# Layer 0 transposes x as it lands and applies its inverse norm behind the projection; x, identity and a gain share one tensor

## The chip, the cores and the metric

The kernel runs on one core of a Trainium2 chip. The metric is the device time of one execution in microseconds (us); lower is better.

## The reference

Four residual layers over 256 tokens of width 1024, everything in float32. Each layer is a token mixer (forgetting attention in layers 0 and 3, chunk attention with a position bias in layer 1, sliding-window attention with sinks in layer 2), a gated MLP with a causal convolution, and a gated per-layer embedding. What matters here is the beginning of layer 0:

```python
def rms_norm(x, g):
    xf = x.astype(jnp.float32)
    y = xf * lax.rsqrt(jnp.mean(xf * xf, axis=-1, keepdims=True) + EPS)
    return (y * g.astype(jnp.float32)).astype(x.dtype)

    h = rms_norm(x, attn_norm[i])
    # fox_mixer
    proj = h @ w_in
    q = rms_norm(proj[..., :D].reshape(B, S, N_HEADS, HEAD_DIM), qn)
    k = rms_norm(proj[..., D:2 * D].reshape(B, S, N_HEADS, HEAD_DIM), kn)
    v = proj[..., 2 * D:3 * D].reshape(B, S, N_HEADS, HEAD_DIM)
    log_f = jax.nn.log_sigmoid((proj[..., 3 * D:] + b_f).astype(jnp.float32))
```

The inverse norm of a token is one number per row of x, so it can be multiplied in before the projection or behind it; the gain belongs to the columns of x and so to the contraction.

## The kernel before

**Arithmetic.** A float32 product is made of three products of rounded operands: each operand is split into a rounded part (`hi`, float32r) and the rest (`lo`), and PE adds hi x hi, hi x lo and lo x hi (`three`, L1409 to L1411). So every weight is rounded by ACT (`split_hi`, L460) and its rest is made by DVE (`split_lo`, L805); the same is done to the transposed activations hT.

**Weights.** They come as units of 128 x 2048 (1 MB) in the order of use, each as two halves of 128 x 1024. SP loads halves into the ring `w_raw` of 4; a slot is free when DVE has made the rest of the half in it (`lo_ready`, the loop at L432 to L436). `w_hi` and `w_lo` are rings of 4 units.

**Order.** There is no scheduler. Each engine has its instructions in the order in which its function is written, and semaphores join them. An engine waits at the first instruction whose semaphore is late, with everything behind it.

**Start of layer 0.** SP issues the two halves of x's first token tile, the identity, `gain0` (the first norm's gain, transposed), the two halves of unit 0, x's second token tile and unit 1 (L425 to L430). ACT squares x with a sum per row (`square`, L486); POOL makes the inverse norm `rstd` from it (`norm_rstd`, L1256, L1249, L1251); DVE multiplies x by it into `tok` (`normalise`, L847); PE transposes `tok` into PSUM banks (`transpose_tok`, L1419); ACT rounds the banks into `hT_hi` with the gain as a scale (`round_hT`, L497), DVE makes the rest `hT_lo` (`rest_hT`, L859). Then PE projects: the first q and k blocks (units 0 and 1, units 2 and 3; 12 matmuls of 128x512 per unit and token tile), first for token tile 0, with the transposes of tile 1 between unit 1 and unit 2, then for tile 1.

**Behind the projection.** An item is one 128x512 block of q or k for one token tile. ACT copies it out of its bank (`evacuate_item`, L575) and squares it (L578), DVE sums the squares by heads (L927), POOL makes the inverse norm of each head and scales the item (`item_rstd` L1249 and L1251, `scale_item` L1316), PE transposes it (L1502), ACT and DVE split it (L563, L977). Layer 0's first evacuation also waits for `gainT`, which POOL scales (L1274) once `small` has landed; POOL issues p, wf, gainT, bf and small itself, behind its part of the first norm (L1263 to L1269). The forget gate takes its columns `wf` by 16 matmuls (L1527) right behind the transposes of item 0; DVE adds the bias (`gate_in`, L1001 and L1003), ACT takes exponential and logarithm (L597 to L601), DVE sums along the tokens. PE takes item 3 only behind `gate_in`. The blocks of v are copied by L592 with rests by L989.

## Time and profile before

| | |
|---|---|
| median of 3 runs | 1325.91 us (1325.15 to 1328.22) |
| profiled execution | span 1323.4 us from its first to its last instruction; the listed runs' median lies 2.5 us above that span |
| PE busy | 1294.3 us, 98% |
| DVE, ACT, POOL busy | 1016.9, 875.2 and 461.1 us |
| chain that ended last | PE 88%, DVE 6%, POOL 2%, ACT 2%, issue 1%, DMA 1% |
| DMA | 232.39 MB, mean 176 GB/s |

The profile comes from one execution. "Busy" counts an engine's instructions without semaphore waits, branches and DMA issues. Matmuls are pipelined and their ends are modelled: a matmul of 128x512 in a stream is listed with some 0.39 us though one starts every 0.23 us. A span of zero waiting on PE therefore doesn't mean that other engines don't matter, but an idle stretch in its row is real.

### The profile page before, as it was taken

The page shows a single profiled execution, that of the slowest core. Times are in us where ns is not written, and L with a number is a line of the kernel's source. Part 1 is how long each engine was busy: PE and PEld are TensorE (multiplying, and loading weights), DVE is VectorE, ACT ScalarE, POOL GpSimd, SP SyncE. Part 2 cuts the span into 40 slices and gives each one's busy share as a digit, 9 for nine tenths or more (in the row PEclk, how much of TensorE's full clock was granted, in tenths as well). Part 3 has the DMA queues.
Part 4 walks back from the last instruction along what each step waited for, and adds up shares of the span by engine and source line. Part 5 has one row for each costly group of instructions (what it writes and reads, how often), then busy time and mean ns, then how long its engine had stood idle before and what let it go on. Part 6 is the DMA issues. An engine that isn't in the chain of part 4 may idle for free.

```text
span 1323.4 us, 22052 instructions
## 1 busy us (share of the span) xinstructions
PE 1294.3 (98%) x6916; PEld 1092.4 (83%) x6916; DVE 1016.9 (77%) x1621; ACT 875.2 (66%) x1569; POOL 461.1 (35%) x520
## 2 busy tenths in 40 slices
PE   6999999999999999999998899999999999999998
PEld 5888888888888888888876688888888888888886
DVE  5877898955777788885588888887476888888745
ACT  6777777744667677774466867776366776777533
POOL 3741245410275225550036315552014621555300
PEclk9999999999999999999998999999999999999999
DMA  7634555564664455556452265556456435555651
GB/s 261 228 115 131 175 192 189 188 220 162 208 225 140 151 176 190 190 190 208 165 178 64 80 223 190 183 188 218 159 184 206 133 124 177 189 190 190 208 174 64
DMA packets 64602, 232.39 MB, mean 176 GB/s; under 512 B 7472, under 2 KB 7600, under 8 KB 64528
## 3 DMA queue, kind: packets, MB, share of 16 engines
q1 hardware_dynamic: 61632, 221.35, 50.7%
q0 software_dynamic: 2896, 10.08, 2.4%
q8 instruction: 43, 0.70, 0.2%
q14 instruction: 31, 0.25, 0.1%
HBM read 230.35 MB, written 1.05 MB: 175 GB/s over the span
## 4 chain that ended last, share of the span: by engine, by line
PE 88%; DVE 6%; POOL 2%; ACT 2%; issue 1%; DMA 1%; SPq 0%; POOLq 0%; DVEq 0%; ACTq 0%
PE bank L1433 25%; PE bank L1683 25%; PE bank L1686 12%; PE bank L1409 6%; PE bank L1411 5%; PE bank L1410 5%; PE bank L1448 4%; DVE w_lo L805 2%; PE bank L1580 2%; PE bank L1603 1%; PE bank L1419 1%; PE bank L1502 1%; DVE tok L849 1%; DMA w_raw<-weights 1%; ACT tok L486 1%
## 5 line engine op out<-in xcount | busy, mean ns | idle before, releaser
L805 DVE TENSOR_TENSOR w_lo<-w_raw,w_hi 128x1024 fp32r<-128x1024 f32 x418 | 544.4, 1321 | 109.6 <-ACT w_hi L460 108.0
L460 ACT ACTIVATE w_hi<-w_raw 128x1024 fp32r<-128x1024 f32 x418 | 429.9, 1053 | 140.9 <-PE bank L1433 106.3
L1683 PE MATMUL bank<-hT,w_hi 128*128 128x512 f32 x1408 | 444.7, 396 | 0.0
L1686 PEld LDWEIGHTS bank<-hT,w_lo 128*128 128x128 f32 x1408 | 264.5, 188 | 59.7
L1686 PE MATMUL bank<-hT,w_lo 128*128 128x256 f32 x1408 | 281.8, 278 | 0.0
L1397 POOL TENSOR_TENSOR gT_lo<-gate_c,gT_hi 128x256 f32 (+1 forms) x88 | 172.2, 1956 | 201.4 <-ACT gT_hi L757 201.4
L1683 PEld LDWEIGHTS bank<-hT,w_hi 128*128 128x128 f32 x1408 | 216.6, 189 | 4.0 <-issue 1.1
L1409 PE MATMUL bank<-w_hi,hT 128*128 128x512 f32 (+1 forms) x336 | 134.2, 399 | 3.9 <-DVE hT L859 3.1
L1256 POOL TENSOR_TENSOR ssq<-ssq 128x1 f32<-128x1 f32 x24 | 7.3, 303 | 370.9 <-ACT tok L486 370.9
L1411 PE MATMUL bank<-w_hi,hT 128*128 128x512 f32 (+1 forms) x336 | 130.2, 388 | 0.0
L1410 PE MATMUL bank<-w_lo,hT 128*128 128x512 f32 (+1 forms) x336 | 130.2, 387 | 0.0
L1433 PE MATMUL bank<-w_hi,hT 128*128 128x512 f32 x384 | 108.1, 392 | 0.0
L764 ACT ACTIVATE cross_c<-bank 128x512 f32<-128x512 f32 x88 | 52.7, 599 | 70.1 <-PE bank L1686 70.1
L1433 PE MATMUL bank<-w_hi,gT_lo 128*128 128x512 f32 x320 | 98.6, 389 | 0.0
L1433 PE MATMUL bank<-w_hi,gT_hi 128*128 128x512 f32 x320 | 98.5, 389 | 0.0
L1395 POOL TENSOR_TENSOR gate_c<-gate_c,up_c 128x256 f32<-128x256 f32 x88 | 67.1, 763 | 90.1 <-ACT gate_c L752 89.0
L1433 PE MATMUL bank<-w_lo,gT_hi 128*128 128x512 f32 x320 | 98.5, 389 | 0.0
L1205 DVE TENSOR_TENSOR both_c<-bank,cross_c 128x512 f32<-128x512 f32 x88 | 60.9, 692 | 48.9 <-ACT cross_c L764 48.3
L771 ACT ACTIVATE gate_c<-both_c,conv_sb 128x256 f32<-128x256 f32 x88 | 53.0, 602 | 57.6 <-DVE both_c L1205 57.6
L1215 DVE SCALAR_TENSOR_TENSOR gate_c<-both_c,conv_sb,gate_c 128x255 f32<-128x255 f32 (+1 forms) x176 | 84.3, 479 | 8.8 <-ACT up_c L773 7.7
L1215 DVE SCALAR_TENSOR_TENSOR up_c<-both_c,conv_sb,up_c 128x255 f32<-128x255 f32 (+1 forms) x176 | 88.1, 500 | 0.0
L1433 PEld LDWEIGHTS bank<-w_hi,hT 128*128 128x128 f32 x384 | 70.8, 188 | 14.6
(162 smaller groups left out, 1983.0 us busy)
## 6 DMA issues: line engine op xcount, KB each, us to landing
w_raw<-weights SPq DMA_DIRECT2D x418, 512.0 KB, 3.5
gain<-gains POOLq DMA_DIRECT2D x11, 512.0 KB, 4.1
rel<-rel_in POOLq DMA_DIRECT2D x8, 256.0 KB, 3.6
x<-x_in SPq DMA_DIRECT2D x4, 256.0 KB, 5.3
out<-x SPq DMA_DIRECT2D x4, 256.0 KB, 2.0
p_end<-p_in POOLq DMA_DIRECT2D x3, 256.0 KB, 5.1
consts<-consts_in POOLq DMA_DIRECT2D x1, 392.0 KB, 5.1
conv_sb<-conv POOLq DMA_DIRECT2D x1, 352.0 KB, 3.9
```

The costliest lines, as they stand in the source:

```text
L460: nc.scalar.activation(w_hi[:, slot, q * HALF:(q + 1) * HALF], w_raw[:, raw, :], ACT.Copy).then_inc(hi_ready, 1)
L805: nc.vector.tensor_tensor(w_lo[:, slot, cols], w_raw[:, half(q)[0], :], w_hi[:, slot, cols].bitcast(F32), ALU.subtract).then_inc(lo_ready, 1)
L1205: nc.vector.tensor_tensor(both_c[:], up_banks(L, slot)[:, :, 0:SEQ], cross_c[:], ALU.add).then_inc(up_sum, 1)
L1215: ins = nc.vector.scalar_tensor_tensor(buf[:, b, lag:SEQ], both_c[:, side, 0:SEQ - lag], c[:, 4 * side + tap:4 * side + tap + 1], buf[:, b ...
L1395: nc.gpsimd.tensor_tensor(gate_c[:, b, :], gate_c[:, b, :], up_c[:, b, :], ALU.mult).then_inc(prod_done, 1)
L1397: nc.gpsimd.tensor_tensor(gT_lo[:, k, :], gate_c[:, b, :], gT_hi[:, k, :].bitcast(F32), ALU.subtract).then_inc(gT_ready, 1)
L1409: nc.tensor.matmul(out_ap, l_hi, r_hi, start=start, stop=False, skip_group_check=True)
L1410: nc.tensor.matmul(out_ap, l_hi, r_lo, start=False, stop=False, skip_group_check=True)
L1411: return nc.tensor.matmul(out_ap, l_lo, r_hi, start=False, stop=stop, skip_group_check=True)
L1433: last = nc.tensor.matmul(banks[2 * t + b][:, :], l[:, c, ts], w[:, slot, col:col + 512], start=(c == 0 and l is left_hi and w is w_hi), s ...
L1683: nc.tensor.matmul(up_banks(L, slot)[:, side, :], w_hi[:, *at(side)], hT[:, c, :, :], start=c == 0, stop=c == KC - 1, skip_group_check=True)
L1686: last = nc.tensor.matmul(up_banks(L, slot)[:, side, 0:SEQ], w_lo[:, *at(side)], hT_hi[:, c, :], start=False, stop=c == KC - 1, skip_group ...
```

## The change

It has four parts, all in layer 0. The first norm's gain, the identity and x lie in one SBUF tensor `first_in` and one DRAM tensor, so that SP's first DMA brings the gain, the identity and the first half of x's first tile. PE transposes x itself, without the inverse norm. The inverse norm comes in where q, k, v and the forget gate leave their banks, as the scale of ACT's instructions (and of DVE's for the rest of v); for the squares it is first multiplied by 1/8 on POOL (`rstd_sq`), and for the gate, whose tokens lie along the free axis, PE transposes it in two instructions and DVE multiplies by it. And the order at the start of ACT and DVE is written anew, with the squares behind unit 1.

Of the diff, without the declarations, the semaphores that go and the mere renaming of `ident[:]`:

```diff
@@ -81,6 +81,8 @@
...
 CUM_LO = 32
+
+X_AT = KC + P + 8
...
 PAIRS = HEADS // 2
@@ -169,17 +171,17 @@
...
         w_lo = sb("w_lo", [P, RING, UNIT], F32R)
-        x = sb("x", [P, TT, D])
+        first_in = sb("first_in", [P, X_AT + TT * D])
+        gain0, ident = first_in[:, 0:KC], first_in[:, KC:KC + P]
+        x = first_in[:, X_AT:X_AT + TT * D].rearrange("p (t d) -> p t d", t=TT)
         tok = sb("tok", [P, TT, D])
...
         gain = sb("gain", [P, D])
-        ident = sb("ident", [P, P])
         consts = sb("consts", [P, C_END])
...
         gainT = sb("gainT", [P, DEPTH, 2])
-        gain0 = sb("gain0", [P, KC])
         conv_sb = sb("conv_sb", [P, DEPTH, FC, 8])
...
         wf_hi, wf_lo = wf[:, :, :, 0:HEADS], wf[:, :, :, 2 * HEADS:3 * HEADS]
@@ -421,11 +423,8 @@
...
                 for b in range(2):
-                    c = slice(b * 512, (b + 1) * 512)
-                    sp.dma_start(x[:, t, c], x_in[t * P:(t + 1) * P, c]).then_inc(x_landed[2 * t + b], 16)
-                if t == 0:
-                    sp.dma_start(ident[:], ident_in).then_inc(ident_landed, 16)
-                    sp.dma_start(gain0[:], gain0_in).then_inc(gain0_landed, 16)
+                    c = slice(X_AT * (t or b) + t * D + b * 512, X_AT + t * D + (b + 1) * 512)
+                    sp.dma_start(first_in[:, c], first_ins[:, c]).then_inc(x_landed[2 * t + b], 16)
                 for g in range(t * 2, t * 2 + 2):
...
             turns = 2 * UNITS // RAW
@@ -492,7 +491,6 @@
...
                     if n == 0:
-                        act.wait_ge(gain0_landed, 16)
                         for k in range(4 * b, 4 * b + 4):
...
                                                        row_bank(0, t, b)[:, (k - 4 * b) * P:(k - 4 * b + 1) * P],
@@ -536,16 +534,16 @@
...
+            for b in range(2):
+                round_hT(0, 0, parts=(b,))
+                split_hi(0, 0, half_of(0), first=True, halves=(b,))
+            split_hi(1, 1, half_of(1), first=True)
             square(0, 0)
-            for b in range(2):
-                split_hi(0, 0, half_of(0), first=True, halves=(b,))
-                round_hT(0, 0, parts=(b,))
-            split_hi(1, 1, half_of(1), first=True)
             square(0, 1)
             split_hi(2, 2, half_of(2), first=True)
-            split_hi(3, 3, half_of(3), first=True, halves=(0,))
-            round_hT(0, 1)
-            split_hi(3, 3, half_of(3), first=True, halves=(1,))
+            for b in range(2):
+                round_hT(0, 1, parts=(b,))
+                split_hi(3, 3, half_of(3), first=True, halves=(b,))
             act.wait_ge(wf_landed, 16)
@@ -572,10 +570,14 @@
...
                         act.wait_ge(qk_tr, n - 2)
-                    nc.scalar.activation(qn[:, n % 3, 0:cols], src[:, 0:cols], ACT.Copy).then_inc(raw_ready, 1)
+                    if L == 0:
+                        act.wait_ge(rstd_sq_ready, t + 1)
+                    nc.scalar.activation(qn[:, n % 3, 0:cols], src[:, 0:cols], ACT.Copy,
+                                         scale=1.0 if L else rstd[:, t:t + 1]).then_inc(raw_ready, 1)
                     if n:
                         act.wait_ge(hsum_ready, n)
-                    nc.scalar.activation(sq[:, 0:cols], src[:, 0:cols], ACT.Square, scale=HD ** -0.5).then_inc(sq_ready, 1)
+                    nc.scalar.activation(sq[:, 0:cols], src[:, 0:cols], ACT.Square,
+                                         scale=HD ** -0.5 if L else rstd_sq[:, t:t + 1]).then_inc(sq_ready, 1)
                     if BLOCKS[m][blk][0] == "kv":
...
                         for twice in range(2):
@@ -839,13 +842,9 @@
...
                 dve.wait_ge(rstd_ready, 2 * n + t + 1)
-                if n:
-                    dve.wait_ge(gain_landed, 16 * n)
+                dve.wait_ge(gain_landed, 16 * n)
                 for b in range(2):
                     c = slice(b * 512, (b + 1) * 512)
-                    if n == 0:
-                        nc.vector.tensor_scalar(tok[:, t, c], x[:, t, c], rstd[:, t:t + 1], None, ALU.mult).then_inc(tok_ready, 1)
-                        continue
                     nc.vector.scalar_tensor_tensor(tok[:, t, c], x[:, t, c], rstd[:, t:t + 1], gain[:, c],
@@ -894,21 +893,14 @@
...
-            dve.wait_ge(x_landed[0], 16)
-            dve.wait_ge(x_landed[1], 16)
-            normalise(0, 0)
-            dve.wait_ge(gain0_landed, 16)
             for b in range(2):
+                rest_hT(0, 0, parts=(b,))
                 split_lo(0, 0, half_of(0), halves=(b,))
-                rest_hT(0, 0, parts=(b,))
             split_lo(1, 1, half_of(1))
-            dve.wait_ge(x_landed[2], 16)
-            dve.wait_ge(x_landed[3], 16)
-            normalise(0, 1)
             split_lo(2, 2, half_of(2))
-            split_lo(3, 3, half_of(3), halves=(0,))
-            rest_hT(0, 1)
-            split_lo(3, 3, half_of(3), halves=(1,))
+            for b in range(2):
+                rest_hT(0, 1, parts=(b,))
+                split_lo(3, 3, half_of(3), halves=(b,))
             dve.wait_ge(wf_hi_ready, 1)
@@ -986,7 +978,11 @@
...
                         cols = slice(c * 512, (c + 1) * 512)
-                        ins = nc.vector.tensor_tensor(v_lo[:, t, cols], src[:, :], v_hi[:, t, cols].bitcast(F32), ALU.subtract)
+                        if L == 0:
+                            ins = nc.vector.scalar_tensor_tensor(v_lo[:, t, cols], src[:, :], rstd[:, t:t + 1],
+                                                                 v_hi[:, t, cols].bitcast(F32), ALU.mult, ALU.subtract)
+                        else:
+                            ins = nc.vector.tensor_tensor(v_lo[:, t, cols], src[:, :], v_hi[:, t, cols].bitcast(F32), ALU.subtract)
                     else:
...
                             at = lambda a: a[:, t, 0:256].rearrange("p (h c d) -> p h c d", c=2, d=HD)[:, :, twice, :]
@@ -997,6 +993,17 @@
...
                     k = L // 3
+                    if L == 0:
+                        dve.wait_ge(f_done, 1)
+                        own.inc(nc.vector.tensor_copy(fe[:], aux[1][0:HEADS, SEQ:2 * SEQ]))
+                        own.inc(nc.vector.tensor_scalar(fmin[:], aux[1][2 * HEADS:3 * HEADS, 0:SEQ], 0.0, None, ALU.add))
+                        own.wait()
+                        own.inc(nc.vector.tensor_tensor(fz[:], aux[1][0:HEADS, 0:SEQ], fmin[:], ALU.add))
+                        own.wait()
+                        own.inc(nc.vector.tensor_tensor(fmin[:], fz[:], fe[:], ALU.mult))
+                        own.wait()
+                        nc.vector.tensor_scalar(fz[:], fmin[:], bf[:, 0:1], None, ALU.add).then_inc(f_z, 1)
+                        return
                     dve.wait_ge(f_done, k + 1)
...
                     own.wait()
@@ -1260,6 +1268,9 @@
...
             norm_rstd(0)
+            for t in range(TT):
+                pool.wait_ge(rstd_ready, t + 1)
+                nc.gpsimd.tensor_scalar(rstd_sq[:, t:t + 1], rstd[:, t:t + 1], HD ** -0.5, 1.0, ALU.mult, ALU.mult).then_inc(rstd_sq_ready, 1)
             pool.dma_start(p_raw(0), p_in[0]).then_inc(p_landed, 16)
...
             pool.dma_start(gainT[:], gainT_in).then_inc(small_landed, 16)
@@ -1413,11 +1424,14 @@
...
                 for b in range(2):
-                    pe.wait_ge(tok_ready, 4 * n + 2 * t + b + 1)
+                    if n:
+                        pe.wait_ge(tok_ready, 4 * (n - 1) + 2 * t + b + 1)
+                    else:
+                        pe.wait_ge(x_landed[2 * t + b], 16)
                     for c in range(4):
...
                         last = nc.tensor.transpose(row_bank(n, t, b)[:, c * P:(c + 1) * P],
-                                                   tok[:, t, k * P:(k + 1) * P], ident[:])
+                                                   (tok if n else x)[:, t, k * P:(k + 1) * P], ident)
                     last.then_inc(tr_done, 1)
...
             def rows_unit(first, k, count, t, left_hi, left_lo, banks, chunks=(0, 1)):
@@ -1520,6 +1533,11 @@
...
                     k3 = L // 3
+                    if L == 0:
+                        pe.wait_ge(rstd_ready, TT)
+                        for t in range(TT):
+                            nc.tensor.transpose(aux[1][0:HEADS, SEQ + t * P:SEQ + (t + 1) * P],
+                                                       rstd[:, t:t + 1].to_broadcast([P, HEADS]), ident)
                     pe.wait_ge(wf_zero, 1)
...
                     for k in range(KC):
@@ -1779,17 +1797,16 @@
...
         "weights": np.stack(units).reshape(UNITS, P, 2, HALF).transpose(0, 2, 1, 3).reshape(2 * UNITS, P, HALF),
-        "x_in": a["x"][0],
+        "first_ins": np.concatenate([a["attn_norm"][0].reshape(KC, P).T, np.eye(P, dtype=np.float32), np.zeros((P, 8), np.float32),
+                                     a["x"][0].reshape(TT, P, D).transpose(1, 0, 2).reshape(P, TT * D)], 1),
         "p_in": a["p"][:, 0].reshape(DEPTH, SEQ, 2, P).transpose(0, 3, 2, 1),
         "gains": np.stack([a[k][L] for L in range(DEPTH) for k in ("attn_norm", "ffn_norm", "ple_norm")]),
-        "gain0_in": a["attn_norm"][0].reshape(KC, P).T,
         "smalls": np.concatenate([np.stack(heads).ravel(), a["sinks"].ravel()]),
...
         "rel_in": a["rel_bias"][0][dist].transpose(0, 2, 1),
-        "ident_in": np.eye(P, dtype=np.float32),
         "consts_in": constants(),
...
     nc = bacc.Bacc("TRN2", target_bir_lowering=False, num_devices=1)
```

The first place where the order moves is the start of ACT's program, up to the last half of unit 3. L486 (of before) and L485 (of the change) are the squares of x, L460 and L459 the rounding of a weight half, L497 and L495 the rounding of hT. Before:

```order
L486 ACTIVATE tok,ssq<-x 128x512 x2
L460 ACTIVATE w_hi<-w_raw 128x1024
L497 ACTIVATE hT<-bank,gain 128x128 x4
L460 ACTIVATE w_hi<-w_raw 128x1024
L497 ACTIVATE hT<-bank,gain 128x128 x4
L460 ACTIVATE w_hi<-w_raw 128x1024 x2
L486 ACTIVATE tok,ssq<-x 128x512 x2
L460 ACTIVATE w_hi<-w_raw 128x1024 x3
L497 ACTIVATE hT<-bank,gain 128x128 x8
L460 ACTIVATE w_hi<-w_raw 128x1024
```

Now:

```order
L495 ACTIVATE hT<-bank,first_in 128x128 x4
L459 ACTIVATE w_hi<-w_raw 128x1024
L495 ACTIVATE hT<-bank,first_in 128x128 x4
L459 ACTIVATE w_hi<-w_raw 128x1024 x3
L485 ACTIVATE tok,ssq<-first_in 128x512 x4
L459 ACTIVATE w_hi<-w_raw 128x1024 x2
L495 ACTIVATE hT<-bank,first_in 128x128 x4
L459 ACTIVATE w_hi<-w_raw 128x1024
L495 ACTIVATE hT<-bank,first_in 128x128 x4
L459 ACTIVATE w_hi<-w_raw 128x1024
```

The four squares stand together behind the fourth weight half, and the first group of hT stands ahead of all weights.

The second place is the start of DVE's program over the same stretch, first before:

```order
L847 TENSOR_SCALAR tok<-x,rstd 128x512 x2
L805 TENSOR_TENSOR w_lo<-w_raw,w_hi 128x1024
L859 SCALAR_TENSOR_TENSOR hT<-bank,gain,hT 128x128 x4
L805 TENSOR_TENSOR w_lo<-w_raw,w_hi 128x1024
L859 SCALAR_TENSOR_TENSOR hT<-bank,gain,hT 128x128 x4
L805 TENSOR_TENSOR w_lo<-w_raw,w_hi 128x1024 x2
L847 TENSOR_SCALAR tok<-x,rstd 128x512 x2
L805 TENSOR_TENSOR w_lo<-w_raw,w_hi 128x1024 x3
L859 SCALAR_TENSOR_TENSOR hT<-bank,gain,hT 128x128 x8
L805 TENSOR_TENSOR w_lo<-w_raw,w_hi 128x1024
```

and now:

```order
L858 SCALAR_TENSOR_TENSOR hT<-bank,first_in,hT 128x128 x4
L808 TENSOR_TENSOR w_lo<-w_raw,w_hi 128x1024
L858 SCALAR_TENSOR_TENSOR hT<-bank,first_in,hT 128x128 x4
L808 TENSOR_TENSOR w_lo<-w_raw,w_hi 128x1024 x5
L858 SCALAR_TENSOR_TENSOR hT<-bank,first_in,hT 128x128 x4
L808 TENSOR_TENSOR w_lo<-w_raw,w_hi 128x1024
L858 SCALAR_TENSOR_TENSOR hT<-bank,first_in,hT 128x128 x4
L808 TENSOR_TENSOR w_lo<-w_raw,w_hi 128x1024
```

The four scalings of x are gone, and hT's first group stands ahead of the first weight half.

## Rows read from the trace of the kernel before

**Rows 1.** The page's first part: engine, busy us (share of the span), instructions.

```profile
PE 1294.3 (98%) x6916; PEld 1092.4 (83%) x6916; DVE 1016.9 (77%) x1621; ACT 875.2 (66%) x1569; POOL 461.1 (35%) x520
```

**Rows 2.** Waits of PE, 12 to 300 us: total, times, longest.

```profile
PE bank L1409 <- DVE hT L859: 3.1, 1, 3.1
PE bank L1409 <- DVE w_lo L805: 0.8, 1, 0.8
```

**Rows 3.** Timeline, SP's first issues: start us, us, engine, line, operation.

```profile
0.75 0.87 SPq L425 DMA_DIRECT2D x<-x_in  x2
1.67 0.42 SPq L427 DMA_DIRECT2D ident<-ident_in  x1
2.13 0.43 SPq L428 DMA_DIRECT2D gain<-gain_in  x1
2.61 0.91 SPq L430 DMA_DIRECT2D w_raw<-weights  x2
```

**Rows 4.** Windows: busy us by engine, granted clock, DMA share, GB/s.

```profile
4.00:5.00 1.00, 0.00 (x0) 0.00 (x0) 0.00 (x0) 1.00 (x3) 0.00 (x0) 1.00 0.54 122
```

**Rows 5.** Timeline, compute engines, 3 to 20 us.

```profile
3.97 0.63 ACT L486 ACTIVATE tok<-x 128x512 f32<-128x512 f32 x1 [1.95 <-DMA x<-x_in]
...
7.40 1.94 PE L1419 MATMUL bank<-ident,tok 128*128 128x128 f32 x8 [7.40 <-DVE tok L847]
8.91 1.06 ACT L460 ACTIVATE w_hi<-w_raw 128x1024 fp32r<-128x1024 f32 x1 [3.60 <-DMA w_raw<-weights]
...
10.07 1.22 DVE L805 TENSOR_TENSOR w_lo<-w_raw,w_hi 128x1024 fp32r<-128x1024 f32 x1 [2.42 <-ACT w_hi L460]
...
11.21 1.12 DVE L859 SCALAR_TENSOR_TENSOR hT<-bank,gain,hT 128x128 fp32r<-128x128 f32 x4
...
12.48 0.77 PE L1409 MATMUL bank<-w_hi,hT 128*128 128x512 f32 x1 [3.13 <-DVE hT L859]
...
19.74 1.03 PE L1419 MATMUL bank<-ident,tok 128*128 128x128 f32 x8
```

**Rows 6.** The chain that ended last, 14 to 26 us: start us, us, what.

```profile
14.00 1.06 ACT w_hi L460
15.06 1.24 ACT tok L486 x4
...
17.92 1.02 DVE tok L847 x2
18.94 3.48 DVE w_lo L805 x3
22.42 2.07 DVE hT L859 x8
...
25.68 0.50 PE bank L1409
```

**Rows 7.** The same chain further on, transposes of items 0, 1 and 3.

```profile
38.26 0.44 PE bank L1502 x4
...
40.56 0.44 PE bank L1502 x4
...
52.40 0.44 PE bank L1502 x4
```

**Rows 8.** Timeline of POOL, 17 to 39 us.

```profile
17.74 0.79 POOL L1263 DMA_DIRECT2D p_end<-p_in  x1
...
20.62 0.57 POOL L1269 DMA_DIRECT2D small<-smalls  x1
27.91 0.59 POOL L1274 TENSOR_SCALAR gainT<-gainT 128x1 f32<-128x1 f32 x3 [6.72 <-DMA small<-smalls]
...
37.18 1.75 POOL L1316 TENSOR_TENSOR qn<-qn,hrstd 128x512 f32<-128x512 f32 x1
```

**Rows 9.** Timeline, forget gate: DVE's first instruction, ACT's first.

```profile
46.24 0.47 DVE L1001 TENSOR_SCALAR fmin<-bank,bf 16x256 f32<-16x256 f32 x1
...
47.19 0.42 ACT L597 ACTIVATE fe<-fz 16x256 f32<-16x256 f32 x1 [2.58 <-DVE fz L1003]
```

17 lines of the change are left out of this document (9 added, 8 removed).

## The prediction

> **What bounds the kernel now.** Four views, in this order. The page's first part says that TensorE (PE) is busy in 98% of the span [rows 1]. The waits of PE alone say where the rest lies: between 12 us and 300 us there are two waits, 3.1 us before the first projection matmul and 0.8 us for a rest `w_lo` of the weights, and after that none for 274 us [rows 2]. So from 25.68 us on PE is the bound, and it starts late: what the change is worth is read in the first 41 us, and whatever lead PE then has it keeps, because its later waits lie in layers that the change does not touch.
>
> The third view is the order of time. SP issues x, x, ident, gain, then the first weights [rows 3], and the DMA engines are only 0.54 busy between 4 and 5 us [rows 4]. ACT squares x from 3.97 us, the transposes run at 7.40 us after the normalisation, ACT rounds the first half unit of weights at 8.91 us when it lands, and DVE makes its rest at 10.07 us. The order on DVE puts the rest of hT (4 instructions, about 1.04 us) behind that, so PE starts at 12.48 us [rows 5]. The reader should see two things there: the inverse norm was finished well before the weights landed, so the normalisation hardly delays anything, and what ends the wait at 12.48 us is one 1.04 us piece of DVE work that could have been done earlier.
>
> The fourth view is the chain: the fourth weight half is rounded at 14.00 us, then come the squares of token tile 1 (1.24 us), the inverse norm, two scalings (1.02 us), three rests of weights in 3.48 us (1.16 each), eight pieces of hT in 2.07 us, one more rest, and PE resumes at 25.68 us [rows 6]. This chain, not the start at 12.48, sets when PE is free of waits.
>
> **Part by part.** I name the weight halves by unit and half: 1.1 is the second half of unit 1.
>
> *Loads.* Two issues go (ident and gain), 0.94 us of SP [rows 3]; the first x transfer grows by the identity, gain and padding. The first weights are issued 0.94 us earlier. Whether they land so much earlier depends on the engines: the gap of rows 4 says that there was free bandwidth just then. Bounds 0 and 1.3 us; I take 0.8 us, near the issue time, for all weights of the first batch: half 0.0 lands at 8.1 us, 1.1 at 13.2 us. The rows of x now start at multiples of 10,816 bytes in place of 4,096 in the source. No row here shows such a transfer. The Trainium skill ("DMA: Bandwidth & Descriptors", How a descriptor splits into AXI transactions) says that a descriptor that does not begin on a 256-byte boundary fetches bytes that it throws away: for rows of 2,048 bytes that would be some 5% of the x traffic, an estimate from that page, and by it the lead below would be 0.5 instead of 0.6 us. Nothing else here uses this.
>
> *Start of PE.* The transposes no longer wait for squares, inverse norm and scaling: they run at about 4.3 us, and hT's first half is complete before the weights. PE then starts at 8.1 + 1.06 + 0.1 + 1.22 + 0.1, about 10.6 us, against 12.48 us: 1.9 us earlier. This is the number that the change shows first and it does not survive: PE will catch up with the weights.
>
> *The chain to the last half unit.* DVE loses four scalings (two of them, 1.0 us, on this chain), but ACT now has all four squares (2 x 1.24 us) behind half 1.1 and ahead of half 2.0; before, the first two lay in idle time at 3.97 us. Half 1.1 is rounded from 13.2 us, ACT is free at 14.2, the squares end about 16.65, half 2.0 is rounded by 17.7, DVE starts its rest at 17.8. From there DVE has four rests of 1.16 and two groups of hT of 1.04 in a row: 4.64 + 2.07, and 0.1 to PE: 24.6 us. Before: 25.68. **Lead 1.1 us** (0.8 from the loads, 0.3 from the order). With 0 and 1.3 us for the loads it is 0.3 and 1.6 us. PE will show new waits for rests of units 2 and 3 of 1.5 to 2 us in all where it had one of 0.8.
>
> *The half-rate stretch.* The transposes at 7.40 us took 1.94 us for 8, those at 19.74 us 1.03 us [rows 5]: PE begins at the lower of its rates (1.2 against 2.4 GHz), though the granted clock column reads 1.00 throughout. That happens in both kernels. Its length can vary, but the waits for units 2 and 3 swallow up to about 3 us of it in the new kernel. I cost it at nothing; without that cover it would be half of the added length.
>
> *Two more transposes for the gate.* The inverse norm is transposed for 16 heads just before the forget-gate matmuls: two at the 0.11 us of an item's transposes (4 in 0.44) [rows 7], 0.2 us of PE that nothing hides. Lead 0.9 us.
>
> *The GpSimd queue.* This is where I expect part of the gain to go. POOL issues p, wf, gainT, bf and small only after the inverse norm of tile 1, at 17.74 us; small is issued at 20.62, and only at 27.91 can gainT be scaled, on which ACT's first evacuation of q waits. From there POOL works without a gap to the scaling of item 1 (the first k tile), 37.18 + 1.75 = 38.93 us [rows 8], and PE takes that item at 40.56 us [rows 7]: 1.53 us of slack with a hop of 0.1. Now the last square ends at about 16.7 instead of 16.3 us (15.06 + 1.24) [rows 6], and two scalings of the inverse norm by 1/8 stand ahead of the issues, 0.2 us each by the 0.59 us for three of the same form [rows 8]. So the chain is 0.9 us later: item 1 is ready at 39.9 us, PE comes for it at 40.56 - 0.9 = 39.7. It waits 0.2 to 0.3 us, and **the lead left is 0.6 us**. Bounds for this shift: 0.3 us (small lands in a quieter moment) to 3 us (it meets the weight loads that now run at 19 to 22 us).
>
> *The gate on DVE.* Three more instructions of 16x256, by 0.47 each at most and with their waits 1.0 to 1.4 us. ACT waits for the result (2.58 us of idle before it already), so what stands behind on ACT shifts by as much: two copies, items 4 and 5, the cumulative sum. PE takes item 3, which also waits for this result, at 52.40 us, while the result was there at 47.2 [rows 9, 7]: 5 us of cover. No cost. If the cover were gone it would be 1 us.
>
> *Scales on the evacuations.* q, k and v of layer 0 take a per-row scale on the same instructions, 20 on ACT, at the same size; v's 4 rests on DVE become three-operand ones. They lie beside PE. Nothing.
>
> *Sum.* 0.8 + 0.3 - 0.2 - 0.3 = 0.6 us less. The profiled execution's span is 1323.4 us; the median of the runs is 1325.91 us, 2.5 us above it, which I take as what lies around the span and leave as it is. Forecast 1322.8 us of span, **1325.3 us**. About 0.2%, 2.7 us, is what a measurement of this kernel can tell from no change, and the three runs before already spread by 3.1 us.
>
> **The rivals.**
> *Lead kept whole.* The POOL chain stays within its slack, and the loads come 1 us or more earlier: 0.9 to 1.8 us gained, 1324.1 to 1325.0 us. For it: the gap of rows 4. Against it: two instructions and the squares really do stand ahead of the issues. Chance 0.25.
> *Loads bound by bandwidth.* The change doesn't bring the weights earlier at all: lead 0.3 - 0.2 = 0.1 us, 1325.8 us. For it: after 5 us the engines are full. Chance 0.15.
> *Slower through the small load.* The loads of the GpSimd queue, issued 0.9 us later, run against weights and land 2 to 4 us later. It decides from a shift of 1.53 us of item 1: PE then waits at 40.56 for shift minus 1.53, so with 3.5 us it is 2.0 us slower, 1327.9 us. For it: small took over 6 us from issue to use, the longest of its queue, for 0.26 MB. Chance 0.15, of which a third above 2.7 us, helped by the spread of runs.
> *Nothing left on PE's side but something of the whole program.* Tiles behind x move by 32 bytes and the rate at the start differs from run to run; that might give 3 us either way. Chance 0.10.
> My forecast, 0.2 to 0.9 us gained with a short wait for item 1, has 0.35.
>
> **The numbers.** The likeliest case gives 1325.3. The range goes from 1323.6 (lead kept, plus the spread of the runs) to 1327.2 (the slow rival at a shift of 2.8 us); the rest of the last two rivals is left out, about 2 in 10. A third of the slow rival and half of the last give slower by over 0.2% 0.08; the upper end of the kept lead together with the spread, and the other half of the last, give faster 0.12; 0.80 within.
>
> **What would show it.** In the changed profile: transposes near 4.3 us; first weights rounded at 8.1 (if 8.9, the loads step is wrong); PE's first matmul at 10.6; four squares in a row near 14 to 16.7; PE free of waits from 24.6; small's use at 28.8; item 1 transposed at about 40.0 after a short wait for POOL. The prediction is wrong if PE resumes later than 25.7 us, if PE waits for qn by more than 1.5 us, or if a wait appears between 41 and 300 us.

## The result, and the profile after

Five runs of the changed kernel have a median of 1336.37 us (1335.08 to 1337.68), five of the kernel before 1325.17 us. The ratio is 1.0086, 95% interval 1.0075 to 1.0096: **11.2 us slower**, where 0.6 us faster was forecast. The profiled execution has a span of 1335.9 us, 12.5 more than before.

The front of the kernel first, since the forecast was worked out there. Timeline of all engines, start us, us, engine, line, operation, in the changed kernel:

```profile
0.75 0.87 SPq L427 DMA_DIRECT2D first_in<-first_ins  x2
1.67 0.90 SPq L429 DMA_DIRECT2D w_raw<-weights  x2
...
3.78 1.97 PE L1433 MATMUL bank<-first_in 128*128 128x128 f32 x8 [3.78 <-DMA first_in<-first_ins]
...
6.79 1.06 ACT L459 ACTIVATE w_hi<-w_raw 128x1024 fp32r<-128x1024 f32 x1 [0.72 <-DMA w_raw<-weights]
...
9.16 0.79 PE L1420 MATMUL bank<-w_hi,hT 128*128 128x512 f32 x1 [3.41 <-DVE w_lo L808]
...
16.77 2.17 POOL L1273 TENSOR_SCALAR rstd_sq<-rstd 128x1 f32<-128x1 f32 x2
...
21.77 0.56 POOL L1280 DMA_DIRECT2D small<-smalls  x1
...
23.89 0.50 PE L1420 MATMUL bank<-w_hi,hT 128*128 128x512 f32 x1 [0.51 <-DVE w_lo L808]
```

Against [rows 3, 5, 6] the transposes run at 3.78 instead of 7.40 us, the weights are rounded at 6.79 instead of 8.91, and PE is free of waits for weights at 23.89 instead of 25.68 us. That is a lead of 1.8 us, more than the forecast's 1.1. Part of what the front lost again is in the waits of PE, 12 to 300 us (total, times, longest), which answer to [rows 2]:

```profile
PE bank L1515 <- POOL qn L1327: 1.1, 1, 1.1
PE bank L1420 <- DVE w_lo L808: 0.8, 2, 0.5
```

No wait in the rest of 300 us explains 12 us. PE did not wait more, it was busy longer. The page's first part says so (engine, busy us, share, instructions), beside [rows 1]:

```profile
PE 1308.4 (98%) x6918; PEld 1094.2 (82%) x6918; DVE 1016.9 (76%) x1620; ACT 876.9 (66%) x1569; POOL 464.0 (35%) x522
```

14.1 us more of PE for two more instructions. The groups by line give it away. Before (line, engine, operation, tiles, shapes, count | busy us, mean ns | idle before):

```profile
L1683 PE MATMUL bank<-hT,w_hi 128*128 128x512 f32 x1408 | 444.7, 396 | 0.0
L1686 PE MATMUL bank<-hT,w_lo 128*128 128x256 f32 x1408 | 281.8, 278 | 0.0
...
L1433 PE MATMUL bank<-w_hi,gT_lo 128*128 128x512 f32 x320 | 98.6, 389 | 0.0
L1433 PE MATMUL bank<-w_hi,gT_hi 128*128 128x512 f32 x320 | 98.5, 389 | 0.0
L1433 PE MATMUL bank<-w_lo,gT_hi 128*128 128x512 f32 x320 | 98.5, 389 | 0.0
```

and in the changed kernel:

```profile
L1701 PE MATMUL bank<-hT,w_hi 128*128 128x512 f32 x1408 | 440.0, 392 | 0.0
L1704 PE MATMUL bank<-hT,w_lo 128*128 128x256 f32 x1408 | 283.4, 279 | 0.0
...
L1447 PE MATMUL bank<-w_lo,gT_hi 128*128 128x512 f32 x320 | 100.6, 396 | 0.0
L1447 PE MATMUL bank<-w_hi,gT_lo 128*128 128x512 f32 x320 | 100.6, 396 | 0.0
L1447 PE MATMUL bank<-w_hi,gT_hi 128*128 128x512 f32 x320 | 100.5, 395 | 0.0
```

The same instructions on the same data, in lines that the diff does not touch: each group of 320 in the down projection took 2.0 to 2.1 us longer, and the first group of the up projection 4.7 us less. I read the distance from the start of one matmul to the start of the next in both traces as a median: for matmuls that move 512 columns of weights it went from 0.227 to 0.231 to 0.235 us, for the up projection's (which move hT) from 0.233 to 0.229, and for its 256-column ones from 0.115 to 0.117. The loss grows with every layer. PE lags behind before by 1.5 us at 133 us, 4.3 at 462, 8.7 at 772 and 12.5 at its last matmul. Not all of it is spacing: this is the slowest of the five runs, and between 638 and 779 us it lost 4.1 us, where e1 below, with spacings about as slow, lost 1.2. In that stretch the granted clock was at its lower level (1.2 GHz) for part of 690 to 695 us (mean 0.66) and of 750 to 760 us (0.83), and in both at 1.00 in before. By that comparison some 3 us of this one profile's 12.5 are clock (an estimate).

What the diff changes for these matmuls is only where the tiles lie. In SBUF, hT moved by 576 bytes (144 columns of gain0, identity and padding ahead of x) and gT by 64 (576, less the 544 of identity and gain0, which no longer stand behind hT, plus 32 for `rstd_sq`). w_hi and w_lo stayed. By the addresses of the program, hT and gT lay a multiple of 256 bytes from w_hi and w_lo before (81,920 and 120,064 bytes from w_hi), and 64 bytes off such a multiple after.

### The profile page after: what moved, and what is told of

It is laid out like the page before. It is cut to its first block, busy times and chain, and to the rows that moved or that the text cites. A ratio compares the mean times of both kernels' runs of the same rounds, so it can differ in the third digit from the quotient of the medians.

```text
span 1335.9 us, 22048 instructions
## 1 busy us (share of the span) xinstructions
PE 1308.4 (98%) x6918; PEld 1094.2 (82%) x6918; DVE 1016.9 (76%) x1620; ACT 876.9 (66%) x1569; POOL 464.0 (35%) x522
## 4 chain that ended last, share of the span: by engine, by line
PE 91%; DVE 3%; POOL 2%; DMA 1%; issue 1%; ACT 1%; SPq 0%; DVEq 0%; POOLq 0%; ACTq 0%
PE bank L1447 28%; PE bank L1701 24%; PE bank L1704 12%; PE bank L1420 5%; PE bank L1421 5%; PE bank L1422 5%; PE bank L1462 5%; PE bank L1598 2%; PE bank L1433 1%; PE bank L1621 1%; DMA w_raw<-weights 1%; PE bank L1515 1%; DVE w_lo L808 1%; DMA small<-smalls 0%; ACT w_hi L459 0%
## 5 line engine op out<-in xcount | busy, mean ns | idle before, releaser
L459 ACT ACTIVATE w_hi<-w_raw 128x1024 fp32r<-128x1024 f32 x418 | 429.6, 1052 | 144.6 <-PE bank L1447 114.4
L1701 PE MATMUL bank<-hT,w_hi 128*128 128x512 f32 x1408 | 440.0, 392 | 0.0
L1420 PE MATMUL bank<-w_hi,hT 128*128 128x512 f32 (+1 forms) x336 | 136.6, 407 | 4.2 <-DVE w_lo L808 4.2
L1422 PE MATMUL bank<-w_hi,hT 128*128 128x512 f32 (+1 forms) x336 | 132.4, 394 | 0.0
```

The lines of the kernel that those rows point to most:

```text
L459: nc.scalar.activation(w_hi[:, slot, q * HALF:(q + 1) * HALF], w_raw[:, raw, :], ACT.Copy).then_inc(hi_ready, 1)
L1420: nc.tensor.matmul(out_ap, l_hi, r_hi, start=start, stop=False, skip_group_check=True)
L1422: return nc.tensor.matmul(out_ap, l_lo, r_hi, start=False, stop=stop, skip_group_check=True)
L1701: nc.tensor.matmul(up_banks(L, slot)[:, side, :], w_hi[:, *at(side)], hT[:, c, :, :], start=c == 0, stop=c == KC - 1, skip_group_check=True)
```

## Experiments on the placement

Theory A, as it stood for e1 to e4: the place of hT and gT paces the matmuls, fast on a multiple of 128 bytes and slow 64 bytes past one. Rival B: the new instructions and the new order of layer 0 cost the time. Rival C: stretches of lower clock in layer 2. A pad is an unused tile; it computes nothing.

**e1**, the changed kernel with hT and gT on multiples of 128 bytes again (their distance to the weights is then 128 off a multiple of 256):

```diff
-X_AT = KC + P + 8
+X_AT = KC + P + 24
```

> The changed kernel with 16 more columns of padding in first_in, so that hT, gT and the attention tiles start on a multiple of 128 bytes again, as in the kernel before; nothing else differs. Theory A (placement: since the change hT and gT start 64 bytes past a multiple of 128, and matmuls with 512 columns of weights then start every 0.233 us instead of 0.227, some 2,700 of them): ratio to before within 0.998 to 1.002, about 1325.6 us, mean listed duration of the matmuls of the down projection back to 0.389 from 0.396 us. Rival B (the new order and the new instructions of layer 0 cost the time): stays at 1.007 to 1.009, near 1336 us. Rival C (clock stretches in layer 2): anywhere between, with the half-rate stretches telling.

Measured: 1337.02 us, ratio 1.0087 (1.0073 to 1.0101). No gain: theory A in this form fell, and the time is the one that rival B gave. Alignment to 128 bytes does nothing.

**e2, e3, e4**, the kernel before with pads of 64 bytes:

```diff
+        sb("pad_h", [P, 16])                 # e2 and e4
         hT = sb("hT", [P, KC, 2, SEQ], F32R)
+        sb("pad_g", [P, 16])                 # e4
         gain = sb("gain", [P, D])
 ...
+        sb("pad_g", [P, 16])                 # e3
         with ExitStack() as ffn:
```

> The kernel before with one unused tile of 64 bytes ahead of hT, so that hT, gT and all tiles behind move by 64 bytes; nothing of the change. A: slower by 0.8% to 1.0%, about 1336 to 1338 us, matmuls of the down projection at 0.396 us, those of the up projection (weights stationary, hT moving) at 0.392. B and C: no difference, 1325 us.

> The kernel before with the 64 bytes ahead of gT and the attention tiles only; hT stays on its multiple of 128. A: only the 960 matmuls with gT stationary slow down by 6 ns, with a little from attention: plus 5 to 8 us, 1331 to 1333 us. B: no difference.

> The kernel before with 64 bytes ahead of hT and 64 behind it, so that hT alone (and the gap) is off its multiple of 128, gT on one. A: some 1,700 matmuls with hT stationary slow down by 6 ns (plus 10 us), the 2,816 of the up projection with hT moving gain 4 ns in half of them and lose 1 ns in the others (minus 4 us): plus 4 to 7 us, 1329 to 1332 us. B: no difference.

Measured: e2 1333.72 us, ratio 1.0058 (1.0044 to 1.0072); e3 1331.38, 1.0042 (1.0027 to 1.0058); e4 1334.66, 1.0066 (1.0050 to 1.0081). In e2 one unused tile of 64 bytes, with nothing else changed, makes the unchanged program 0.58% slower. That is less than the 0.8% to 1.0% expected, but neither B nor C can give it: they expected no difference. Its groups are those of the changed kernel:

```profile
L1684 PE MATMUL bank<-hT,w_hi 128*128 128x512 f32 x1408 | 440.0, 392 | 0.0
L1687 PE MATMUL bank<-hT,w_lo 128*128 128x256 f32 x1408 | 283.4, 279 | 0.0
...
L1434 PE MATMUL bank<-w_lo,gT_hi 128*128 128x512 f32 x320 | 100.6, 396 | 0.0
```

In e3 only gT moved, and only gT's matmuls became slower (0.233 us); those with hT stayed at 0.227 and the up projection at 0.233. e4 was meant to move hT alone but also left gT 128 bytes off its multiple, and both were slow, so that it came out above its 1329 to 1332 us; it adds only that 128 off costs gT's matmuls as 64 does.

Only now was the theory put that fits all five, A2: what counts is the distance between the tiles that a matmul reads, modulo 256 bytes, with 0 fast. (The placements run so far had distances of 0, 64 and 128; the 192 that e5's expectation names was in none of them.)

**e5**, the changed kernel with hT and gT again at multiples of 256 from the weights:

```diff
-X_AT = KC + P + 8
+X_AT = KC + P + 56
```

**e6**, the kernel before with everything moved by 128 bytes together:

```diff
+        sb("pad_w", [P, 32])
         w_raw = sb("w_raw", [P, RAW, HALF])
```

> The changed kernel with 48 more columns of padding in first_in, so that hT and gT have again the distance to w_hi and w_lo that they had before: a multiple of 256 bytes. Theory A2 (the rate of the 512-column matmuls depends on where stationary and moving operand lie to each other, modulo 256 bytes; the runs so far have 0 fast and 64, 128 and 192 slow): the 0.389 us of the down projection's matmuls return, ratio to before 0.998 to 1.002, and the difference to the changed kernel, 10 to 12 us, is all placement. Rival B2 (the new instructions and order of layer 0 slow the rest in some way): stays near 1336 us.

> The kernel before with an unused tile of 128 bytes ahead of all its tiles: every address moves by 128 bytes, no distance changes. A2 (distance): no difference, 1325 us. Rival A3 (the address itself, 128 modulo 256 being the good one): slower by 0.4% to 0.9%, like the kernels in which hT and gT moved.

Measured: e5 1328.83 us, ratio 1.0024 (1.0015 to 1.0034), spacings back at 0.227, 0.233 and 0.115; e6 1325.28, 1.0003 (0.9994 to 1.0012). So it is the distance and not the address, at least for a common shift of 128 bytes, and **0.62% of the 0.86%, some 8 us, is placement alone**. The other 0.24%, 3.2 us, lies above the 0.2% that A2 allowed, and it still is on the wrong side. Some 0.7 us of it is placement too: e5 brought hT and gT back but not the small tiles `p_hi` and `p_lo` (224 bytes further on than in before), and the 96 matmuls of 512 columns that multiply p by weights are spaced 0.234 us in e5 against 0.227 in before (in e7, e8 and e12 as well). The rest is something else.

**e9 and e15** ask which pair of tiles counts. (e9 moved w_lo by 64 bytes and everything behind it by 256.)

```diff
-        w_lo = sb("w_lo", [P, RING, UNIT], F32R)
-        x = sb("x", [P, TT, D])
+        sb("pad_w", [P, 16])                 # e9 and e15
+        w_lo = sb("w_lo", [P, RING, UNIT], F32R)
+        sb("pad_x", [P, 48])                 # e9 only
+        x = sb("x", [P, TT, D])
```

> The kernel before with w_lo alone moved by 64 bytes (every other large tile keeps its distance from w_hi as a multiple of 256). Pair theory (a matmul is paced by the distance between its own stationary and moving tiles): all 944 matmuls of 512 columns with w_lo moving are spaced 0.233 instead of 0.227 us, those with w_hi moving stay at 0.227, in the up projection only the 256-column ones with w_lo stationary change (0.115 to 0.117); in sum 5.7 + 1.4 us, about 1332.3 us. Neighbour theory (what counts is the tile whose weights are loaded while another moves): the 512-column matmuls of the up projection, during which w_lo is loaded, go from 0.233 to 0.229, which gives 5.5 us back: about 1326 us.

> The kernel before with a pad of 64 bytes between w_hi and w_lo: w_lo, hT and gT keep their distances from each other, w_hi alone is 64 bytes off from all. Own-pair theory: matmuls with w_lo moving keep 0.227, up's 256-column ones (w_lo stationary) 0.115, those with w_hi moving go to 0.233 and up's 512-column ones to 0.229; in sum +8.5 - 5.5 = 3 us, 1328.3. If, as the run with w_lo moved suggests, a matmul also feels the weights before and after it: w_lo's matmuls slow down as well, 0.230 or more, up stays at 0.233, and the time is above 1332 us.

Measured: e9 1339.41 us, ratio 1.0099 (1.0084 to 1.0113); e15 1337.49, 1.0086 (1.0071 to 1.0101). Both theories of e9 fell, and the own-pair theory's 1328.3 us in e15 too. Groups of e9:

```profile
L1685 PE MATMUL bank<-hT,w_hi 128*128 128x512 f32 x1408 | 445.5, 395 | 0.0
L1688 PE MATMUL bank<-hT,w_lo 128*128 128x256 f32 x1408 | 285.9, 280 | 0.0
...
L1435 PE MATMUL bank<-w_hi,gT_hi 128*128 128x512 f32 x320 | 100.2, 394 | 0.0
L1435 PE MATMUL bank<-w_hi,gT_lo 128*128 128x512 f32 x320 | 100.0, 394 | 0.0
L1435 PE MATMUL bank<-w_lo,gT_hi 128*128 128x512 f32 x320 | 100.0, 394 | 0.0
```

w_hi and gT are still a multiple of 256 apart, and yet their matmuls slowed from 98.5 to 100.2 us; the up projection lost on its second group (281.8 to 285.9) and did not win on the first. e15 reads the same (443.4 and 285.3 us in up; 100.4, 99.8 and 99.5 in down, w_lo's too). A matmul's own pair does not explain this. That it also feels the tiles of its neighbours in the order was e15's other expectation, and its signs came: w_lo's matmuls at 0.232 us in the down projection, the up projection's first group at 0.233, over 1332 us. It is supported by that and by no run made for it alone. The working rule that all placements run here fit: with w_hi, w_lo and the activations all a multiple of 256 apart, rows of weights move at 0.227; with any of them off, at 0.228 to 0.237. Which access of which instruction meets which is open, and so is whether it is two accesses that meet at all.

**e10 and e11** use the one place where a distance helps. The kernel before, with hT written some bytes further on for the second norm of each layer (`n % 3 == 1`), so that only the up projection reads it there:

```diff
-        hT = sb("hT", [P, KC, 2, SEQ], F32R)
+        hT_all = sb("hT", [P, KC * 2 * SEQ + 16], F32R)      # 8 in e11
+        hT = hT_all[:, 0:KC * 2 * SEQ].rearrange(...)
+        hT_up = hT_all[:, 16:16 + KC * 2 * SEQ].rearrange(...)
 ...
+        sb("pad_g", [P, 48])                                 # 56 in e11
         gain = sb("gain", [P, D])
 ...
-    w_hi[:, *at(side)], hT[:, c, :, :],
+    w_hi[:, *at(side)], hT_up[:, c, :, :],
```

> The kernel before, with hT written 64 bytes further on for the layers' second norm alone, so that the up projection reads it there and all other matmuls find hT and gT at a distance of a multiple of 256 from w_hi and w_lo. If only the distance sets the spacing: up projection 0.229 and 0.117 us as in the changed kernel, all others 0.227 as before; 5.5 less 1.3 us, so 4.2 us faster than before, about 1321 us (ratio 0.997). If the spacing of the up projection depended on something else that the earlier pads moved as well: no difference, 1325.3.

> As the one before with 32 bytes instead of 64. If any distance off a multiple of 256 does it: again about 1321 us and 0.229 and 0.117. If the step is 64 bytes: no difference from before, 1325.3 and 0.233 and 0.115.

Measured: e10 1322.49 us, ratio 0.9969 (0.9958 to 0.9981); e11 1323.59, 0.9987 (0.9978 to 0.9997). e10 is faster than the kernel before, by as much as the spacing says (the expectation's 0.997), with the same instructions, one operand at another address. Its groups:

```profile
L1687 PE MATMUL bank<-hT,w_hi 128*128 128x512 f32 x1408 | 439.9, 392 | 0.0
L1690 PE MATMUL bank<-hT,w_lo 128*128 128x256 f32 x1408 | 283.3, 279 | 0.0
...
L1437 PE MATMUL bank<-w_hi,gT_hi 128*128 128x512 f32 x320 | 98.6, 389 | 0.0
```

With 32 bytes (e11) the first group falls to 438.3 us but the second rises to 285.8, so it gives about half, which neither of its two theories had expected.

## Experiments on the other 3 us

In e5 PE waits for `qn`, which no profile of the kernel before shows. First its waits, 12 to 300 us:

```profile
PE bank L1515 <- POOL qn L1327: 2.2, 2, 1.5
PE bank L1420 <- DVE w_lo L808: 0.9, 3, 0.5
```

Where that comes from, in the timeline of the changed kernel (DVE and one row of POOL, 46 to 50 us; in before the gate began at 46.24 and ACT's part of it at 47.19 [rows 9]):

```profile
46.90 0.40 DVE L998 COPY fe<-bank 16x256 f32<-16x256 f32 x1
47.33 0.42 DVE L999 TENSOR_SCALAR fmin<-bank 16x256 f32<-16x256 f32 x1
47.78 0.41 DVE L1001 TENSOR_TENSOR fz<-bank,fmin 16x256 f32<-16x256 f32 x1
...
47.98 1.05 POOL L1327 TENSOR_TENSOR qn<-qn,hrstd 128x512 f32<-128x512 f32 x1
...
48.23 1.07 DVE L1003 TENSOR_TENSOR fmin<-fz,fe 16x256 f32<-16x256 f32 x1
49.34 0.34 DVE L1005 TENSOR_SCALAR fz<-fmin,bf 16x256 f32<-16x256 f32 x1
```

and further on in the same kernel's chain that ended last, to item 5 (start us, us, what):

```profile
49.72 0.42 ACT fe L600
...
55.90 0.46 POOL hsum L1257
...
63.59 1.05 POOL qn L1327
...
64.69 0.66 PE bank L1515 x4
```

The gate takes 2.8 us, from 46.90 to 49.68, where it took 0.92. ACT waits for it, and behind ACT's wait stand the evacuations of items 4 and 5; from item 4's sums on, POOL's steps follow one another with hardly a gap. In before, POOL's timeline and the chain have for item 5:

```profile
60.90 1.04 POOL L1316 TENSOR_TENSOR qn<-qn,hrstd 128x512 f32<-128x512 f32 x1
...
64.25 0.44 PE bank L1502 x4
```

Item 5 was ready at 61.94 us there and is ready at 64.64 now, and PE came for it at 64.25 before (the chain's figure; its timeline has the first transpose at 64.09). The slack was 2.2 to 2.3 us, not the 5 us that I read at item 3.

The 1.07 us is odd beside 0.41 for the same form two rows above. It began while POOL scaled an item (47.98 to 49.03) and ended 0.27 us after it. In e7 POOL had finished its item 0.4 us before, and the same instruction took 0.41. The row above it, with one input from a bank, ran beside POOL too and took 0.41. This agrees with the Trainium skill ("SBUF — State Buffer", Who interferes with whom), by which a VectorE instruction with two SBUF inputs contends with a GpSimd instruction that reads SBUF, and one with at most one does not.

**e7** is e5 with the gate's steps one place later on ACT and DVE, so that items 1, 2 and 4 no longer wait for it:

```diff
 # ACT
-                        gate_logs()
                         copy_items(1, 2)
                         evacuate_item(4)
-                        round_cum()
+                        gate_logs()
                         evacuate_item(5)
+                        round_cum()
 # DVE
-                        gate_sum()
                         rest_items(2)
                         sum_item(4)
-                        rest_cum()
+                        gate_sum()
                         sum_item(5)
+                        rest_cum()
```

**e8** is e7 with tile 0's squares first on ACT, and on POOL the memsets first, wf, small, gainT and bf issued behind tile 0's inverse norm, p behind tile 1's.

```diff
 # ACT
+            square(0, 0)
             for b in range(2):
                 round_hT(0, 0, parts=(b,))
 ...
-            square(0, 0)
             square(0, 1)
 # POOL, in the loop over t, behind rstd_sq
+                if t == 0:
+                    pool.dma_start(wf_raw[:], wf_in)...
+                    pool.dma_start(small[:], ...)...
+                    pool.dma_start(gainT[:], gainT_in)...
+                    pool.dma_start(bf[:], bf_in)...
+                else:
+                    pool.dma_start(p_raw(0), p_in[0])...
```

> As e5, and in addition ACT rounds items 1 and 2 and copies out item 4 before it takes the gate's exponential and logarithm, DVE in the matching order. Theory G (the 2.5 us by which the gate's input comes later on DVE reach PE by way of ACT's queue and POOL, as a wait of 1.1 us for item 5): no wait of PE for item 5, PE some 1 to 1.5 us earlier than in e5 from there on. Rival: item 5 hangs on something else (POOL's queue, ACT's squares), and the wait stays.

> As e7, and in addition the squares of token tile 0 stand ahead of all weights on ACT (it waits for the transposes there), and POOL issues wf, small, gainT and bf behind the inverse norm of tile 0 and p behind that of tile 1. If the four squares behind unit 1 held the chain of weights, PE is free of waits 1.2 us earlier (about 22.9 us) and keeps that, for 1323 us; if the loads of the first 20 us are limited by bandwidth, the earlier small loads take it back and it stays at e7's time.

Measured: e7 1326.45 us, ratio 1.0010 (1.0000 to 1.0019), no wait for item 5 and one of 0.4 us for item 1; e8 1324.51, 0.9996 (0.9988 to 1.0005), no wait for qn at all. By the ratios each step gives some 2 us. In the profiles PE is 2.2 us earlier at 133 us in e7 than in e5, and 0.8 earlier in e8 than in e7; so much of each step is seen, and the rest of the second is within the intervals. Together they bring the time back to the kernel before. e8 did it in another way than its expectation had it: PE was free of waits at 23.79 us against 23.95 in e7, not 1.2 us earlier, and took item 1 at 38.68 against 39.42. In e8's timeline of POOL, with the row of DVE that runs beside the first `rstd_sq`:

```profile
6.30 1.13 DVE L858 SCALAR_TENSOR_TENSOR hT<-bank,first_in,hT 128x128 fp32r<-128x128 f32 x4 [6.30 <-ACT hT L495]
6.56 0.20 POOL L1279 TENSOR_SCALAR rstd_sq<-rstd 128x1 f32<-128x1 f32 x1
...
16.92 0.92 POOL L1279 TENSOR_SCALAR rstd_sq<-rstd 128x1 f32<-128x1 f32 x1
...
18.46 0.91 POOL L1291 TENSOR_SCALAR gainT<-gainT 128x1 f32<-128x1 f32 x3
```

gainT is scaled at 18.46 us without a wait, and no longer at 27.91 [rows 8]. So `small`, issued at 7.47 us behind tile 0, was there in time; issued at 20.62 us in before and 21.77 in the change it cost POOL 6.7 and 5.6 us of waiting.

**e13 and e14** take two parts of the change alone into the kernel before.

```diff
 # e13: the tensor and the four transfers of the change, X_AT = KC + P + 56, and a pad that keeps gT's distance
-                    sp.dma_start(x[:, t, c], x_in[t * P:(t + 1) * P, c])...
-                if t == 0:
-                    sp.dma_start(ident[:], ident_in)...
-                    sp.dma_start(gain0[:], gain0_in)...
+                    sp.dma_start(first_in[:, c], first_ins[:, c])...
 # e14: in gate_in, results overwritten
+                    if L == 0:
+                        own.inc(nc.vector.tensor_scalar(fmin[:], aux[1][2 * HEADS:3 * HEADS, 0:SEQ], 0.0, None, ALU.add))
+                        own.wait()
+                        own.inc(nc.vector.tensor_tensor(fz[:], aux[1][0:HEADS, 0:SEQ], fmin[:], ALU.add))
+                        own.wait()
+                        own.inc(nc.vector.tensor_tensor(fmin[:], fz[:], fz[:], ALU.mult))
+                        own.wait()
```

> The kernel before with the loads of the change alone: gain0, identity and 56 columns of zeros in front of x in one tensor, four transfers in place of six, all distances kept. By my prediction's step the first weights land 0.8 us earlier and, with the old order of the engines, the chain to the last half unit is 0.8 us earlier: 1324.4 us. If the landing is set by the DMA engines and scatters from run to run anyway (profiles so far: first half rounded between 7.4 and 8.9 us with the old loads, 6.2 and 7.8 with the new): 0.8 +- 0.7 us in one profile, and a median of 1324 to 1325.3. If the longer source rows cost something: 1326 or more, first half rounded at 8.9 or later.

> The kernel before with three more 16x256 instructions and their waits in layer 0's gate on VectorE and nothing else (their results are overwritten). Gate theory: ScalarE and GpSimd get to item 5 some 2 us later; GpSimd had it ready 2.3 us before TensorE came for it, so TensorE waits 0 to 1.5 us for it, more the earlier the weights landed: 1325.3 to 1326.5 us, and a wait of TensorE for qn that no profile of the kernel before shows. By my prediction (five us of cover at item 3): 1325.3 and no wait.

Measured: e13 1325.67 us, ratio 1.0000 (0.9991 to 1.0008); e14 1324.88, 0.9998 (0.9989 to 1.0007). Neither part alone moves the time by more than its interval, which for e13 still holds the 0.8 us that it was to gain. In e14 the three instructions added 1.35 us, no wait for qn appeared, and item 5 was scaled at 61.44 and ready at 62.48 us, 1.5 us before PE came. Some 0.5 us of that is the profile: its gate began at 45.42 us, 0.8 earlier than in before, and PE was 0.3 earlier. So the gate alone fits its slack, and the 0.5 us by which the change's gate is longer still would fit into what is left (an estimate). In e5, where the gate also began 1.3 us later than in before (47.57 against 46.24 us) because ACT and POOL came late to items 0 to 3, it did not fit.

What the profiles show of the 3.2 us: at 133 us PE is 1.3 us later in e5 than in before, and 2.0 us later than the mean of the five profiles with the old order and all distances kept (before, e6, e10, e11, e14). The 0.7 us of p's matmuls come on top. So most of it is several delays on one chain that together outgrow 2.3 us of slack, and not one cause; how they divide further no run takes apart, and the last half us is within the interval.

**e13's profile shows why a lead at the front is hard to find in the end.** PE was 1.65 us ahead of before at 133 us, and 0.28 us behind at 772. Between them, in layer 2, the granted clock falls to its lower level (1.2 GHz) and rises again (columns as in [rows 4]). Before:

```profile
700.00:750.00 50.00, 39.10 (x239) 30.71 (x238) 42.29 (x146) 36.43 (x107) 25.15 (x39) 0.86 0.14 47
750.00:800.00 50.00, 50.00 (x264) 42.42 (x263) 41.81 (x61) 35.63 (x59) 9.01 (x15) 1.00 0.60 200
```

and e13:

```profile
700.00:750.00 50.00, 37.66 (x234) 29.10 (x234) 41.62 (x147) 36.20 (x107) 24.41 (x40) 0.88 0.13 43
750.00:800.00 50.00, 50.00 (x259) 42.29 (x258) 40.96 (x57) 34.00 (x56) 8.33 (x14) 0.98 0.61 200
```

PE is busy for only 39.10 and 37.66 us of the first 50, and in e13 the low level reaches past 750 us. Between 638 and 779 us profiles lose 0.2 to 0.4 us against before (e6, e7, e12, e14) or 1.6 to 1.9 (e5, e8, e10, e11, e13), with or without the change. The 1.9 us that e5's profile loses there are thus no sign of a cost of the change. I read this as scatter between executions; one profile must not be read across it.

**e12** puts the pieces together: e8 with the up projection's hT 64 bytes further on, and the padding replaced by small tiles moved ahead of hT.

```diff
-X_AT = KC + P + 56
+X_AT = KC + P + 8
 ...
+        nsink, ssq, rstd, rstd_sq, neghalf   # moved here, ahead of hT
+        hT_all = sb("hT", [P, KC * 2 * SEQ + 16], F32R)
 ...
+        sb("pad_g", [P, 32])
         gain = sb("gain", [P, D])
```

> The changed kernel with the placement, the later gate and the earlier loads and squares of the run before (e8, 1324.5 us), and the up projection reading hT 64 bytes further on. Placement theory: e8 less 4.2 us, about 1320.3 us, ratio 0.9965 to before; the small tiles moved ahead of hT cost nothing. If the parts don't add up: 1322 or more.

Measured: 1320.41 us (1320.2 to 1322.91), ratio 0.9964 (0.9951 to 0.9977). The parts add up, and this is faster than both kernels: 5.6 us under before by the medians of that chip (4.8 by the ratio), and by the medians some 16 under the change, which ran at another time. Nearly all of the gain over before is e10's placement; e8, which has all the rest, is level with before.

## Why the prediction was wrong, by its own steps

*"Nothing left on PE's side but something of the whole program."* This rival, "Tiles behind x move by 32 bytes ... 3 us either way", chance 0.10, is what decided. Its place was named, but its size was a guess that no row gave, and its 32 bytes hold only for small tiles such as those of p: hT and gT, which matter, moved by 576 and 64 bytes. In the sum the term stood at nothing, and the upper end of the range, 1327.2 us, left it out. **This is the step that failed**: placement measured 0.62%, some 8 us, where the sum had 0 and the rival 3. The trace of before has no price per matmul, but it has the count: some 2,900 matmuls with weights moving and 2,816 in the up projection, so that each ns on the former alone is 2.9 us. The runs then showed 6 ns more on the former, and 4 ns less and 1 to 2 ns more on the two halves of the latter. The rival rested on the spread of runs and on no mechanism; that it named the place at all is in part luck.

*"The gate on DVE ... 5 us of cover. No cost."* Wrong twice. The addition was 1.0 to 1.4 us by the forecast and 1.9 us in the run, of which 0.66 is the instruction that ran beside POOL's. And the cover was read at item 3, which waits for this result itself, where the queue behind it on ACT leads to items 4 and 5, with 2.3 us. The prediction lists those items as shifted and does not follow them to PE. One of its three "wrong if" signs came: a wait beyond 41 us, of 1.1 us at 63.6. The other two did not (PE was free at 23.89 us, and no wait for qn was over 1.5 us), so the front and its signs could not have shown the 8 us.

*"rstd_sq ... 0.2 us each."* The two took 2.17 us in the changed kernel, 1.0 and 1.2, while DVE made `w_lo` (16.53 to 18.89 us), both of whose inputs come from SBUF. In e8 the first took 0.20 us beside DVE's L858, one of whose inputs comes from a bank, and the second 0.92 beside `w_lo`. The forecast took the price from three scalings during which DVE was idle. The issue of small was then 1.15 us later (21.77 against 20.62) and not 0.9, but small landed no later: gainT was scaled at 27.91 in both, and item 1 was ready at 39.19 against 38.93 us. So the step "item 1 is ready at 39.9 us" was wrong by 0.7 us. PE's wait for item 1, forecast at 0.2 to 0.3 us, was 0.23 for its weight load in the change and 0.73 in e5; in the change that is luck, since PE came some 0.5 us earlier than forecast and POOL 0.7.

*"Scales on the evacuations ... at the same size ... Nothing."* 0.66 to 0.70 us instead of 0.57 to 0.62: 0.09 each. The Trainium skill ("ScalarE: Activation LUTs", What ACT_TABLE_LOAD costs) has 93 ns for each operand that is a column instead of a constant, and the trace agrees. Two such lie on the chain of every item, and the sum left them out. The first evacuations in before and in the changed kernel:

```profile
28.54 0.60 ACT L575 ACTIVATE qn<-bank 128x512 f32<-128x512 f32 x1 [4.07 <-POOL gainT L1274]
...
28.52 0.69 ACT L575 ACTIVATE qn<-bank,rstd 128x512 f32<-128x512 f32 x1 [2.55 <-POOL gainT L1285]
```

*"0.2 us of PE that nothing hides"*, the gate's two transposes: right. They are listed with 0.38 us, but the gate's first matmul starts 0.57 us behind item 0's first transpose where it was 0.35. PE's lead fell by 0.35 between items 0 and 1; the rest is the wait above.

*Right were the loads and the order.* The first half unit is rounded at 8.19 us on average over the ten profiles with the old loads (7.13 to 8.93) and at 7.16 over the seven with the new (6.22 to 7.83): 1.0 us against 0.8 forecast. PE is free of waits at 25.1 us with the old loads and order (nine profiles) and 23.9 with the new (six, of which two have tile 0's squares first): 1.2 against 1.1. "Transposes near 4.3 us" came at 3.78, "item 1 at 40.0" at 39.24. The scatter between profiles with the same loads is as large as the term. The new waits for units 2 and 3, forecast at 1.5 to 2 us in all, were 0.8. The rows of `first_ins` are 8,768 bytes long and not 10,816 as the prediction says; no run isolates what it costs that x does not start on a 256-byte boundary in them.

*"The half-rate stretch ... nothing."* Right for the start: matmuls of 512 columns started 0.43 us apart until 14.9 us in the change and 15.6 in before, and PE then still waited for `w_lo` at 21.7 and 23.9 us. The stretch in layer 2 has no term in the prediction.
